# Feed-forward stage of a hybrid decoder step: the down projection's weight blocks in a ring of 20 slots, a single-block operand first, a third slot for the h operand, and another GpSimd order in gate/up

## What is computed

```python
xn = rmsnorm(x, p['g_pre_ffn'])
gate = xn @ p['w_gate']
up = xn @ p['w_up']
padded = jnp.concatenate([conv_prev.astype(gate.dtype), gate], axis=1)
conv = p['conv_b'] + sum(padded[:, i:i + t] * cw[i] for i in range(CONV_W))
hdn = jax.nn.gelu(conv) * up
x = x + rmsnorm(hdn @ p['w_down'], p['g_post_ffn'])
conv_new = padded[:, padded.shape[1] - (CONV_W - 1):]
```

## Time and profile before

| what | us |
|---|---|
| median of 3 runs | 3459.91 (3459.48 to 3466.13) |
| the profiled execution, its own time | 3459.59 |
| its span, first to last instruction | 3457.6 |
| gate/up, first pass, tiles 4 to 19 | 2038.05 to 2394.56 |
| gate/up, tiles 23 to 42 and part of 43 | 2479.6 to 2913.3 |
| last tile's K5 to the third down step | 2913.3 to 2968.4 |
| down steps 2 to 55 | 2968.4 to 3447.2 |

### The profile page before, as it was taken

How to read it: one execution, slowest core, us unless ns; L and a number is a source line. 1 busy time by engine, 2 the same in 40 slices (tenths; PEclk the granted TensorE clock), 3 DMA queues, 4 the chain that set the end, 5 groups by cost and what they waited for, 6 DMA issues and landing times. The chain is left out here.

```text
span 3457.6 us, 47005 instructions
## 1 busy us (share of the span) xinstructions
PE 3148.2 (91%) x13945; PEld 2115.6 (61%) x13945; DVE 2335.3 (68%) x2904; ACT 1323.6 (38%) x2249; POOL 1179.2 (34%) x996
## 2 busy tenths in 40 slices
PE   6999985899999999998899599999899998899988
PEld 5787753344444444444787377777677776677666
DVE  6110678987988988994566676667888886344445
ACT  4100113666556556563444332223433332332222
POOL 2000101643444344341144345555355554122112
PEclk9999988999999999999999799999999999999999
DMA  3322234978988988997555233343433334454554
GB/s 116 101 79 67 76 87 118 304 235 281 304 277 284 305 273 288 306 298 242 181 164 151 88 107 105 110 115 109 143 92 96 97 98 126 148 177 163 175 192 167
DMA packets 501235, 591.69 MB, mean 171 GB/s; under 512 B 66191, under 2 KB 308975, under 8 KB 499372
## 3 DMA queue, kind: packets, MB, share of 16 engines
q1 hardware_dynamic: 494094, 574.17, 53.3%
q10 hardware_dynamic: 6912, 15.26, 1.4%
q0 software_dynamic: 32, 0.03, 0.0%
HBM read 484.37 MB, written 103.86 MB: 170 GB/s over the span
## 5 line engine op out<-in xcount | busy, mean ns | idle before, releaser
L2689 PE MATMUL tail_bank<-ffn_xw,ahead_wop 128*128 128x512 f32 x2112 | 530.4, 409 | 72.9 <-DVE ffn_xw L2943 31.6
L2689 PEld LDWEIGHTS tail_bank<-ffn_xw,ahead_wop 128*128 128x128 f32 x2112 | 408.1, 195 | 182.0 <-issue 50.3
L2766 PE MATMUL tail_bank<-ffn_xw,ahead_wop 128*128 128x512 f32 x1848 | 451.0, 405 | 20.8 <-DVE ahead_wop L2957 17.6
L1378 POOL TENSOR_TENSOR att_S<-att_S,att_X 128x512 f32<-128x512 f32 (+3 forms) x256 | 344.7, 1347 | 287.4 <-PE att_bank L1667 216.7
L2766 PEld LDWEIGHTS tail_bank<-ffn_xw,ahead_wop 128*128 128x128 f32 x1848 | 354.7, 193 | 121.1 <-DVE ahead_wop L2957 20.7
L2689 PE MATMUL tail_bank<-gate_xr,ahead_wop 128*128 128x512 f32 x1584 | 381.6, 399 | 16.2 <-DVE gate_work L3030 11.5
L2689 PEld LDWEIGHTS tail_bank<-gate_xr,ahead_wop 128*128 128x128 f32 x1584 | 300.4, 190 | 90.3 <-issue 18.1
L1562 DVE TENSOR_TENSOR att_prod<-att_Kr,att_q_wide 128x1024 f32<-128x1024 f32 x256 | 326.0, 1273 | 5.0 <-DMA att_Kr<-in_cache_k_dram 4.8
L1662 PE MATMUL att_bank<-att_X,att_negtri 128*128 128x512 f32 (+3 forms) x640 | 299.1, 550 | 29.4 <-DVE att_X L1533 28.7
L1567 DVE TENSOR_REDUCE att_z_s<-att_prod 128x16 f32<-128x1024 f32 x256 | 313.3, 1224 | 8.8
L1428 ACT ACTIVATE att_X<-att_bank 128x512 f32<-128x512 f32 (+2 forms) x320 | 171.0, 534 | 257.6 <-PE att_bank L1651 224.3
(11 more groups left out here) (416 smaller groups left out, 5495.9 us busy)
## 6 DMA issues: line engine op xcount, KB each, us to landing
att_Kr<-in_cache_k_dram SPq DMA_DIRECT2D x512, 256.0 KB, 3.7
att_Vr<-in_cache_v_dram SPq DMA_DIRECT2D x488, 256.0 KB, 3.8
hop_dram<-gate_work SPq DMA_DIRECT2D x154, 256.0 KB, 2.6
ahead_wf<-hop_dram SPq DMA_DIRECT2D x56, 704.0 KB, 4.4
ahead_wf<-in_w_gate_dram SPq DMA_DIRECT2D x44, 512.0 KB
ahead_wf<-in_w_up_dram SPq DMA_DIRECT2D x44, 512.0 KB, 5.3
ahead_S<-in_w_down_dram SPq DMA_DIRECT2D x45, 256.0 KB, 4.6
ahead_wf<-in_w_down_dram SPq DMA_DIRECT2D x45, 256.0 KB, 4.6
```

Source lines behind the costliest of these rows:

```text
L1378: pool.tensor_tensor(new[:, r:], old[:, r:], x[:, r:], ALU.add).then_inc(s_part, 1)
L2689: mm = pe.matmul(bank[:, b, :], wop[:, k, w, q], xop(k, x)[:, q], start=(k in (K1, K6, K5) and q == 0 and n == 0), stop=(q == KH - 1 and n ...
L2766: mm = pe.matmul(bank[:, s % 3, :], a_op[s % 2][a][:, p, :], wd_op[:, n % NW, w, :], start=(p == 0 and q == 0), stop=(p == PAIRS_F - 1 and ...
```

## The change

Two things are edited, both in the feed-forward part.

In gate/up POOL's order within a tile becomes `prepare(g+1)`, `finish(g+1)`, `sum_h(g)`, `sum_parts`.

In the down part:
- A weight operand is loaded, summed and split in place in one of 20 slots: raw blocks and split halves share them (stage, S, a part of wf, the 16 slots of xw, and the end of wop). The load of operand n waits for the last use of operand n-20 instead of the split of n-3. For the first 20 it waits only until the memory is free.
- The first two operands change places: operand 0 is now the single-block one, so its 11 blocks need no sum; operand 1 is a pair with a difference.
- The h operand has three slots. Steps 2 and 3 are loaded before the last `store_h`.
- Operand 0's results are now written twice by ACT (two copies per step instead of one), and POOL's eight copies are gone.
- The plan which loads, sums, splits and sample products stand in which step is a table each (LOADS, SUMS, SPLITS); the sums run a step ahead of the splits, and the last two splits of an operand stand in its own first step. In step 0 to 5 ACT copies the turned gate rows before it splits the next h operand.
- In tile 43 the splits are spread otherwise; block 0 is loaded in `body(42)`.

```diff
+                    if not known(g, LASTG - 1):
+                        finish(g + 1, (j + 1) % 2)
                     if j % 2 == 0 and not known(g, 0, 1):
                         sum_h(g, j, h2)
                     if i is not None and j % 2 == 0:
                         sum_parts(i, j // 2)
-                    if not known(g, LASTG - 1):
-                        finish(g + 1, (j + 1) % 2)
...
+        NA = 3
+        a_raw = [raw[:, 0:AW1], raw[:, AW1:2 * AW1], a_far[:]]
...
+        wd_op = ring_slots(stage_r, early["S_r"], early["wf_r"], xw, wop)
+        wd_in = ring_slots(stage, S, wf, xw_raw, early["wop_raw"])
+        NW = len(wd_op)
+        XW0 = 3
+
+        def wd_raw(n, h):
+
+            return wd_in[n % NW][:, 1 - h]
...
-        PAIRED = {0: ((0, 1), (1, 1)), 1: ((1, 1),), 2: ((0, 0), (1, 1)), 3: ((1, 0), (0, 0)), 4: ((1, 0), (1, 1)), 5: ((0, 0),), 6: ((0, 0), (0, 1))}
-        MINUS = (0, 3)
-        NM = OPS * PAIRS_F
+        PAIRED = {0: ((1, 1),), 1: ((0, 1), (1, 1)), 2: ((0, 0), (1, 1)), 3: ((1, 0), (0, 0)), 4: ((1, 0), (1, 1)), 5: ((0, 0),), 6: ((0, 0), (0, 1))}
+        MINUS = (1, 3)
+        LOADS = ((0, 1, 2), (3,), (4, 5), (6,), (7,), (8,), (), (9, 10))
+        SUMS = ((), (0, 1), (2,), (3, 4), (5,), (6, 7), (8,), (9, 10))
+        SPLITS = ((9, 10), (), (0, 1), (2,), (3, 4), (5,), (6, 7), (8,))
...
                 def load_wd(n):
                     i, p = divmod(n, PAIRS_F)
-                    at(sp, wd_lo, n - NWD + 1)
+                    if n >= NW:
+                        i0, p0 = divmod(n - NW, PAIRS_F)
+                        if p0 < PAIRS_F - 1:
+                            sp.wait_ge(wd_used, i0 * (PAIRS_F - 1) + p0 + 1)
+                        else:
+                            sp.wait_ge(acc, (i0 + 1) * STEPS)
+                    elif n >= XW0:
+                        sp.wait_ge(prod, (LASTG - 1) * OPS + min((n - XW0) // 4 + 1 if n < NW - 1 else OPS, OPS))
+                    elif n:
+                        sp.wait_ge(w_lo, LASTG * OPS)
+                        sp.wait_ge(s_made, FT)
+                    else:
+                        sp.wait_ge(x_ready[K3], 1 + KH)
...
+                load_a(2)
+                load_a(3)
                 store_h(LASTG, FT - 2, LASTG % 4, LASTG // 2)
-                sp.wait_ge(h_ready, LASTG)
...
                 for s in range(LASTS):
-                    if s + 2 < LASTS:
-                        load_a(s + 2)
-                    for n in ops_of(s, 8, 8):
-                        load_wd(n)
+                    if 4 <= s + NA < LASTS:
+                        load_a(s + NA)
+                    for n in ops_of(s, LOADS):
+                        if n >= NW - 1:
+                            load_wd(n)
...
                         else:
-                            for n in ((0, 1), (2, 3), (4, 5), (6, 7), (8, 9), (10,), ())[k]:
+                            if k == K7:
+                                split_a(0)
+                            for n in ((0, 1), (2,), (3, 4), (5, 6), (7, 8), (9, 10), ())[k]:
                                 split_wd(n)
-                            if k == K2:
-                                split_a(0)
-                            if k == K3:
+                            if k == K4:
                                 split_a(1)
...
-                    dst = {0: C[:, 0, 1, u, :], 1: C[:, 0, 0, u, :], 3: C[:, 1, 0, u, :]}[i]
-                    act.activation(dst, bank[:, s % 3, :], ACT.Copy, scale=-1.0 if i == 1 else 1.0).then_inc(c_act, 1)
+                    for th, d, sign in {0: ((0, 1, 1.0), (0, 0, -1.0)), 1: ((1, 1, 1.0),), 3: ((1, 0, 1.0),)}[i]:
+                        act.activation(C[:, th, d, u, :], bank[:, s % 3, :], ACT.Copy, scale=sign).then_inc(c_act, 1)
```

More of the change, by code:

```diff
@@ L2266, in stage_ffn, with ring_slots @@
         raw = wf[:].rearrange("p s q k c -> p (s q k c)")
[L2267 to L2271 removed]
+        NA = 3
+        a_raw = [raw[:, 0:AW1], raw[:, AW1:2 * AW1], a_far[:]]
         ring = wop[:].rearrange("p o h k c -> p (o h k c)")
         a_op = [[ring[:, (2 * n + h) * AW1:(2 * n + h + 1) * AW1].rearrange("p (f t) -> p f t", t=P) for h in range(2)] for n in range(2)]
[L2274 to L2275 removed]
+        halves = lambda x: x.rearrange("p (h n) -> p h n", h=2)
+        def ring_slots(first, second, third, most, end):
+            flat = most[:].rearrange("p o h k n -> p (o h k n)")
+            return ([first[:], halves(second[:].rearrange("p s k c -> p (s k c)")),
+                     halves(third[:].rearrange("p s q k c -> p (s q k c)")[:, 2 * AW1:2 * AW1 + 2 * CH])]
+                    + [halves(flat[:, x * 2 * CH:(x + 1) * 2 * CH]) for x in range(16)]
+                    + [halves(end[:].rearrange("p o h k c -> p (o h k c)")[:, 4 * AW1:4 * AW1 + 2 * CH])])
+        wd_op = ring_slots(stage_r, early["S_r"], early["wf_r"], xw, wop)
[4 more added lines that the diff above has]
+            return wd_in[n % NW][:, 1 - h]
         def xop(k, h):
@@ L2382, in samples_of @@
         def samples_of(i, where):
-            return {**{u: (u - 2,) for u in range(2, 7)}, 7: (5, 6, 7), 8: (8, 9, 10)}.get(where, ()) if i + 1 in SAMPLED else ()
+            return ((), (0, 1), (2,), (3, 4), (5,), (6, 7), (8,), (), (9, 10))[where] if i + 1 in SAMPLED else ()
         def sampled_before(n):
@@ L2483, in body @@
+                    if s == 0:
                         for x in range(2):
@@ L2486, in body @@
                             sp.wait_ge(hsum_stored[x], 16 * PAIRS_F * (2 if x == 0 else 1))
+                    if s == 4:
+                        for x in range(2):
+                            sp.wait_ge(hraw_stored[x], 16 * 2 * PAIRS_F)
+                        for x in range(4):
+                            sp.wait_ge(hsum_stored[x], 16 * 2 * PAIRS_F * (2 if x == 0 else 1))
+                    o = ((i * 2 + u // 4) * 4 + u % 4) * P
+                    sp.dma_start(a_raw[s % NA], A["hop"][o:o + P, :]).then_inc(a_loaded[s % NA], 16)
+                def body(g):
+                    if g < LASTG - 2:
+                        weights(g + 2, (g + 2) % FT, g % 2)
+                    if g == LASTG - 2:
                         load_wd(0)
+                    if g == LASTG - 1:
                         load_wd(1)
@@ L2491, in body @@
                         load_a(1)
-                        for n in range(NWD, PAIRS_F):
+                        for n in range(XW0, NW - 1):
                             load_wd(n)
@@ L2765, in _ @@
                         for q, (a, w) in enumerate(((0, 0), (0, 1), (1, 0))):
-                            mm = pe.matmul(bank[:, s % 3, :], a_op[s % 2][a][:, p, :], wd_op[:, n % NW, w, :], start=(p == 0 and q == 0),
+                            mm = pe.matmul(bank[:, s % 3, :], a_op[s % 2][a][:, p, :], wd_op[n % NW][:, w], start=(p == 0 and q == 0),
                                            stop=(p == PAIRS_F - 1 and q == 2), skip_group_check=True)
@@ L2905, in _ @@
                         evacuate(s - 1)
-                    if s and s + 1 < LASTS:
-                        split_a(s + 1)
                     if 1 <= s <= NTG:
@@ L2912, in _ @@
                                        ).then_inc(tails_copied, 1)
+                    if s % STEPS == 0:
+                        for n in ops_of(s, SPLITS):
+                            split_wd(n)
+                    if s and s + 1 < LASTS:
+                        split_a(s + 1)
                     if s and row_of(s - 1) is not None:
                         square(s - 1)
-                    for n in ops_of(s, 0, 5):
-                        split_wd(n)
+                    if s % STEPS:
+                        for n in ops_of(s, SPLITS):
+                            split_wd(n)
                     if s == 6 * STEPS + 2:
@@ L3039, in body @@
                             tt(t1, t1, b(C_B), ALU.add).then_inc(c12_ready, 1)
+                            if last:
+                                split_wd(9)
+                                split_wd(10)
+                                split_a(1)
                             taps(g, f, j, h2)
```

134 lines of the change are left out of this document (60 added, 74 removed).

## The result

The changed kernel takes 3368.33 us (median of 4 runs, 3365.17 to 3376.91), the kernel before 3459.69 beside it. The ratio is 0.9737, with a 95% interval of 0.9715 to 0.9759. The profiled execution took 3369.21, its span 3367.5, which is 90.1 less than before. The forecast, 3400, was 32 too high.

What follows compares the result with a forecast made beforehand. TensorE was taken to lose time waiting in the first pass, the switch and steps 2 to 55, and to be fully busy in the second pass. 3459.6 - 2 (gate/up) - 23 (switch) - 35 (steps) = 3400, range 3368 to 3428.

Steps and rivals of the forecast that it cites:

- Gate/up order: First pass, tiles 4 to 19: POOL's new order only moves the stall from K2 to K4; 2 us won.
- rival 1: First pass: the gate/up stall really goes, part or all of 42.9 us won; 3357 to 3385, chance 0.15.
- my own case: Whole kernel: the forecast itself, 3388 to 3412, chance 0.52.
- Steps 2 to 55: Down projection: 40.0 us lost to late-issued loads and low clock behind them; 35 won, bounds 22 and 39.
- late blocks: Down steps: pairs 9 and 10 wait for slots and land late; 5 of the 40.0 us left as lost.
- the loop: Row steps: block load, y store, finish and previous split chained at about 12 us; 20 slots make it 6 per step.
- Rivals 2 and 3: Down steps: ring late at six operand switches, 3430, chance 0.13; row steps' loop stays, 3422, chance 0.08.
- rival 4: Switch: the queue is slower, 19 blocks being fetched at once beside h; 3415 to 3420, chance 0.05.
- Switch: K5 of tile 43 to step 2: unsummed single blocks and earlier h loads win 23 us, bounds 14 and 27.
- POOL's chain (rival 5): Gate/up, both passes: delayed sum_h makes each pair's K6 sum later; slower, chance 0.04, and 0.03 that it eats the gain.

Runs made afterwards that it cites:

- three experiments more: Changed kernel with part loads before h stores: 3358.28; parts also summed in POOL's idle time: 3359.80; also POOL's sums kept off DVE's taps, last-tile splits moved: 3344.97 us.
- The experiment with the same columns: Changed kernel with both pairs of each double group of sample products put in the same column quadrants instead of different ones: 3375.22 us, ratio 0.9749.

## Why the prediction was right in sign and 32 us too high

**Gate/up order: 2 predicted, 22.1 measured. This is the step that failed.** Pairs were to stay at about 44; they take 41.8 on average. The mechanism was right link by link. Counted from the pair's start, `sum_h` began at 11.9 (I had 12.0), the part loads were issued at 20.5 (20.0), `sum_parts` began at 24.7 (24.2), and from the end of L1738 to K4 it was 4.4 (4.4). Two sizes were wrong. `sum_parts` took 4.06 and not the 5.23 of the earlier trace rows: so L1738 ended at 31.4, not 32.4, and the gap was 2.0. Before, it ran beside DVE's taps; 3.7 later it began as they ended. That this is the reason is likely and not shown: with the parts loaded early it ran beside the taps again, and took 4.54. And I charged the low clock, 1.66, behind every gap; it came behind two of eight. Per pair that is 1.2 + 1.25, over eight pairs 20. What I had called rival 1, with a chance of 0.15, is what the time came out as: 3368 lies in its 3357 to 3385, and outside of the 3388 to 3412 that I gave my own case. It was only a part of the stall that went, though; the whole went with the edits of three experiments more.

**Steps 2 to 55: 35 predicted, 44.3 measured.** Two sizes were wrong. The 5 that I left for late blocks were 0.85 (at 3232.43). And I counted the sample products as 22 times 0.98 in both kernels, though they stand in 14 groups in either. Before, ten groups hold one pair and four hold three, like this one, between two steps of the kernel before:

```profile
3202.13 7.96 PE L2766 MATMUL tail_bank<-ffn_xw,ahead_wop 128*128 128x512 f32 x33
3210.03 0.62 PE L2746 MATMUL tail_bank<-ahead_wf,ffn_hs 128*32 128x512 f32 x2
3210.04 0.62 PE L2746 MATMUL tail_bank<-ffn_stage,ffn_hs 128*32 128x512 f32 x2
...
3210.91 1.03 PE L2746 MATMUL tail_bank<-ahead_S,ffn_hs 128*32 128x512 f32 x4
3211.86 7.96 PE L2766 MATMUL tail_bank<-ffn_xw,ahead_wop 128*128 128x512 f32 x33
```

Three pairs take 1.83, since two of them run side by side (their rows start together); one pair takes 0.98; and the 33 matmuls behind a group take 7.89, not 7.70. So the samples cost 10 x 1.17 + 4 x 2.02 = 19.8 and not 21.6, and 478.8 less 415.8, 19.8 and 1.4 leaves 41.8 lost, not 40.0. In the changed kernel eight groups hold two pairs and six hold one, and each costs 0.98 + 0.19: 14 x 1.17 = 16.4. I had read the new plan in the diff and gave it no price. Together, 41.8 - 0.85 of waits and 19.8 - 16.4 of samples are 44.4. The experiment with the same columns shows why a second pair is free.

The reason that I gave for the row steps, that the ring's lookahead breaks the loop, isn't confirmed. Cutting the lookahead brought waits back in front of sample products alone; taking the third slot away brought none. What is left is the schedule (splits spread over seven of the eight steps, where six of eleven stood in the last one; POOL's norm ahead of its sums) and the raw blocks' own places. These weren't separated, and this stays open. Rivals 2 and 3 didn't occur: 0.85 is all that was awaited between operands, and nothing in the row steps, with two slots for h neither. Nor did rival 4: the queue moved 328 GB/s over the switch, and my rate was 0.30 MB/us, which is 300.

**Switch: 23 predicted, 26.3 measured.** A gap of 2.42 in front of K4 where I had 3, a step 2 that began 28.8 after K5 where I had 30, and nothing late behind it. I had the taps over 21.3 after K5 and the h operand of step 2 landed at 26.7; they were over at 19.9 (2913.6) and it landed at 24.1, 4.1 after its issue. By the experiments, the early h loads are worth 13.6 (9.3 of it in the switch itself, the rest behind it) and the single block 5; the two need not add up, and what remains of the 26 wasn't taken apart.

**POOL's chain (rival 5)** had its condition, later sums, without its price: 31.4 is below the 32.4 of my own sum.

## What to carry to other kernels

When an order is changed on one engine, walk the chain with the durations of the neighbourhood that each instruction moves into, and write the low clock as a chance, not as a fixed surcharge. When a stall vanishes, look at once for the next one on the same loop: here K2's 3.3 became K4's 2.0, that became K7's 1.3 and then 1.05, and only the edit after that reached the matmuls' own time. Where two engines hold each other up, a wait that keeps the one without a deadline away from the other can be worth more than any shorter chain.

## What the runs showed of the hardware that I had not expected

- DVE operations stretch beside POOL's sums. A copy of 2 elements grew from 0.16 to 1.25, two taps from 2.71 to 4.34; with POOL held back they were 2.71 again, and that, with the other edits of its kernel, was worth 10.2 us in the stretch.
- Sample products, which fill 32 of the array's 128 columns, run at the same time in different column quadrants: 8 records in 1.06, and in 1.91 where they share quadrants. The change to and from them costs the following 33 matmuls 0.19.
- A gap of about 2 us is or isn't followed by the lower level of TensorE's clock: the same gap of 2.05 had 7.39 for 24 matmuls behind it once and 5.84 another time, though both stood at the same place of the loop. Over the traces of the experiments the same holds for gaps from 1.8 to 2.4. Gaps of 3.1 and more had it behind them in all rows that were read, gaps of 1.5 and less in the gate/up tiles never.
